# A fused two-block layer: the loads and first products of the ada prologue rearranged

## What is computed

```python
mod = (silu(c) @ w_ada + b_ada)                     # c: 1024, w_ada: 1024 x 6144
shift1, scale1, gate1, shift2, scale2, gate2 = split(mod, 6)
h = rms_norm(x, norm1_w) * (1.0 + scale1) + shift1  # x: 512 x 1024
proj = h @ w_in                                     # first product on h
```

## Time and profile before

| | us |
|---|---|
| median of three runs | 1274.04 |
| lowest and highest | 1273.92, 1275.78 |
| the profiled execution, device time | 1273.12 |
| its span | 1271.2 |
| PE busy | 1221.3 |
| DVE busy | 701.7 |
| ACT busy | 492.0 |

### The profile page before, as it was taken

The page is one execution under the profiler, slowest core; times in us unless marked ns, Lnnn a source line. Parts: engine busy times, 40 slices in busy tenths (PEclk is TensorE's granted clock), DMA queues, the critical chain, the costliest instruction groups (busy, mean ns, idle before and its releaser), DMA issues.

```text
span 1271.2 us, 20461 instructions
## 1 busy us (share of the span) xinstructions
PE 1221.3 (96%) x8672; PEld 994.5 (78%) x8672; DVE 701.7 (55%) x1018; ACT 492.0 (39%) x774; POOL 107.0 (8%) x151
## 2 busy tenths in 40 slices
PE   2899999997999999999999999999999999999998
PEld 2577788787878888888888889798767678888886
DVE  4699878654468544323333457758456546334344
ACT  4543543665246323112222344223446663232232
POOL 4000004621011000000000110000012320000000
PEclk9899999999999999999999999999999999999999
DMA  9666621000222535233322343333231115433311
GB/s 311 219 209 184 219 66 36 3 3 31 74 67 71 163 105 160 81 111 104 100 87 63 86 146 94 100 92 76 41 79 46 34 47 134 115 87 87 114 40 67
DMA packets 150955, 125.62 MB, mean 99 GB/s; under 512 B 16985, under 2 KB 134514, under 8 KB 150737
## 3 DMA queue, kind: packets, MB, share of 16 engines
q1 hardware_dynamic: 147888, 119.88, 31.3%
q0 software_dynamic: 1232, 2.07, 0.5%
q10 hardware_dynamic: 1744, 2.36, 0.5%
HBM read 122.20 MB, written 2.10 MB: 98 GB/s over the span
## 4 chain that ended last, share of the span: by engine, by line
PE 91%; DVE 3%; DMA 2%; ACT 2%; issue 1%; POOL 0%; ACTq 0%; DVEq 0%; POOLq 0%
PE bank L583 56%; PE bank L676 5%; PE bank L825 5%; PE bank L1255 4%; PE bank L1226 4%; PE bank L1289 3%; PE bank L1143 2%; DMA arena<-in_meta_tokens_dram 1%; PE bank L988 1%; PE bank L1117 1%; PE bank L834 1%; PE bank L1176 1%; PE bank L1198 1%; PE bank L1156 1%; PE bank L797 1%
## 5 line engine op out<-in xcount | busy, mean ns | idle before, releaser
L583 PE MATMUL bank<-hsplit,whi 128*128 128x512 f32 (+1 forms) x1872 | 551.9, 379 | 0.7 <-DVE wlo L2005 0.7
L583 PEld LDWEIGHTS bank<-hsplit,whi 128*128 128x128 f32 x1872 | 341.2, 188 | 73.0 <-issue 8.0
L583 PE MATMUL bank<-hsplit,wlo 128*128 128x512 f32 (+1 forms) x936 | 352.3, 376 | 0.0
L2005 DVE TENSOR_TENSOR wlo<-ring,whi 128x2048 fp32r<-128x2048 f32 (+4 forms) x97 | 196.9, 2029 | 178.1 <-ACT whi L1485 177.8
L1485 ACT ACTIVATE whi<-ring 128x2048 fp32r<-128x2048 f32 (+4 forms) x97 | 165.4, 1705 | 129.3 <-DVE xT L2355 53.3
L583 PEld LDWEIGHTS bank<-hsplit,wlo 128*128 128x128 f32 x936 | 175.9, 188 | 33.1
L583 PE MATMUL bank<-a_split,whi 128*128 128x512 f32 x340 | 104.6, 389 | 0.0
L583 PEld LDWEIGHTS bank<-a_split,whi 128*128 128x128 f32 x340 | 63.8, 188 | 13.2
L583 PE MATMUL bank<-a_split,wlo 128*128 128x512 f32 x170 | 66.1, 389 | 0.0
L2034 DVE SCALAR_TENSOR_TENSOR post<-ring,small,post 128x512 f32<-128x512 f32 x77 | 57.9, 752 | 3.1 <-DMA ring<-in_w_ada_dram 0.4
L1426 POOL TENSOR_TENSOR acc<-acc,tb 128x512 f32<-128x512 f32 x12 | 17.7, 1478 | 426.2 <-ACT tb L1723 426.2
(11 more groups left out here) (443 smaller groups left out, 1726.2 us busy)
## 6 DMA issues: line engine op xcount, KB each, us to landing
ring<-in_w_ada_dram SPq DMA_DIRECT2D x24, 1024.0 KB, 5.2
ring<-in_w_in_dram SPq DMA_DIRECT2D x22, 1024.0 KB, 5.3
ring<-in_w_in_dram SPq DMA_DIRECT2D x34, 512.0 KB, 5.1
ring<-in_w_gate_dram SPq DMA_DIRECT2D x11, 1024.0 KB, 5.4
ring<-in_w_up_dram SPq DMA_DIRECT2D x11, 1024.0 KB, 5.2
ring<-in_w_down_dram SPq DMA_DIRECT2D x8, 768.0 KB, 4.9
ring<-in_w_down_dram SPq DMA_DIRECT2D x8, 640.0 KB, 4.5
ring<-in_w_out_dram SPq DMA_DIRECT2D x4, 1024.0 KB, 5.3
```

The costliest lines, as they stand in the source:

```text
L583: last = mm(o[0:m, 0:n], w[:, k, c0:c0 + m], rhs(s, k), start=k + i == 0, stop=k == kn - 1 and i == 2)
L2005: split_lo = splitter(dve, None, lambda lo, src, hi: tt(lo, src, hi, ALU.subtract))
```

## The change

It touches the prologue only.

1. SP starts the load of `x` first, before all panels (ACT started it before). The eight half panels of ada blocks 2, 0, 3 and 1 get buffers of their own (`early_ada`, in memory that is used later) and semaphores of their own, and no longer pass through the ring. The order of SP is `x`, ada 2, ada 0, `qkv0`, ada 3, ada 1, `qkv1`, `qkv2`. `ld_const_rest` comes after `qkv2`.
2. Each of the four sums is shared: DVE takes the first half panel (four steps instead of eight), PE the second. PE takes each 128x128 piece of that half panel as stationary operand, with one column of silu(c) moving, 16 matmuls (`L630` in the changed kernel), and adds DVE's sum with the four matmuls that were there before. `ada_rows` and `ada_turn` are gone.
3. `scale1`, `shift1` and the modulation go by halves of the channels: blocks 2 and 0 for chunks 0 to 3, then blocks 3 and 1 for chunks 4 to 7. PE does ada 3 after chunk 1 of `first_tiles` and ada 1 after chunk 3.
4. `c` is loaded as eight rows of 128, turned by PE, and silu is applied from PSUM.
5. DVE copies chunks 0 to 3 of the transposed `x`, ACT chunks 4 to 7. The work on the meta tokens goes behind the first tiles, the memset of `gates` goes from DVE to POOL.

```diff
+        early_ada = {(i, h): hscratch[:, (2 * n + h) * PANEL:(2 * n + h + 1) * PANEL] for n, i in enumerate((2, 0)) for h in range(2)}
+        early_ada |= {half: C1.take(PANEL) for half in ((3, 0), (3, 1), (1, 0))}
...
+        early_ada[1, 1] = C1b.take(PANEL)
...
-        for i in range(4):
-            ada_panel(i)
...
             def ada(i):
 
                 o = open_tile(pe, "ada", i)
+                if i < 4:
+                    pe.wait_ge(*ada_loaded(i, 1))
+                    for k in range(4):
+                        for c in range(4):
+                            mm(o[:, c:c + 1], ada_half(i, 1)[:, k, c * P:(c + 1) * P], cs[:, 4 + k:5 + k],
+                               start=c + k == 0, stop=False)
                 pe.wait_ge(*done("adaacc", i))
                 for c in range(4):
-                    last = mm(o[:, c:c + 1], adaacc[i % 2][:, c * P:(c + 1) * P], ones[:, 0:1], start=True, stop=True)
+                    last = mm(o[:, c:c + 1], acc_of(i)[:, c * P:(c + 1) * P], ones[:, 0:1], start=i >= 4, stop=i >= 4 or c == 3)
                 last.then_inc(*fill("ada", i))
...
             pe.wait_ge(*arrived("const"))
-            pe.wait_ge(*arrived("x", 2))
+            pe.wait_ge(*arrived("c"))
+            tr(open_tile(pe, "c")[:, 0:KD], c_rows, ident[0:KD, 0:KD]).then_inc(*fill("c"))
+            pe.wait_ge(*arrived("x"))
...
+            ada(2)
+            norm_spread("1", diag)
             pe.wait_ge(*arrived("rows", 20))
...
-            ada(1)
-            norm_spread("1", diag)
...
-            ada_rows(3)
-            ada(2)
-            ada_turn(3)
+            ada(0)
...
-                    first_tiles("qkv0", h_ready("1"), [(("pj", c), P * c, T, hx) for c in range(2)])
+                    first_tiles("qkv0", h_ready("1"), [(("pj", c), P * c, T, hx) for c in range(2)],
+                                between={1: [(ada, 3)], 3: [(ada, 1)]})
+                    meta_columns()
...
+            sp.dma_start(x_in, a["x"][0].rearrange("(b p) f -> p b f", p=P)).then_inc(sem("ld_x"), 16)
+            load_ada(2)
+            load_ada(0)
             for i, (name, kn, width, parts) in enumerate(panels):
+                if name == "qkv1":
+                    load_ada(3)
+                    load_ada(1)
...
-            for k in range(KD):
+            for k in range(KD // 2, KD):
                 act.wait_ge(*filled("x", k))
                 A(xT[:, k, :], bank("x", k)[:, :], ACT.Copy).then_inc(*read("x", k))
...
-            modulate("1", modA1, 0)
+            modulate_half(0)
+            modulate_half(1)
...
+            ada_sum(2)
+            spread("1", diag)
             ada_sum(0)
...
+            normed("1", "xn1")
+            dve.wait_ge(*done("act_vectors", "v1"))
+            scale_half(0)
+            ada_mod(0)
+            split_lo()
+            h_rest("1", range(2))
+            ada_sum(3)
+            h_rest("1", range(2, 4))
             ada_sum(1)
+            scale_half(1)
+            ada_mod(1)
+            h_rest("1", range(4, 8))
```

More of the change, by code:

```diff
@@ L653, in _, with meta_columns @@
             tr(o[:, P:P + V2_N], rows2[0:V2_N, :], ident[0:V2_N, 0:V2_N]).then_inc(*fill("vec"))
[L654 to L661 removed]
+            ada(0)
+            def meta_columns():
+                pe.wait_ge(*arrived("meta"))
+                o = open_tile(pe, "meta")
+                for k in range(KD):
+                    last = tr(o[:, k * META:(k + 1) * META], meta_in[0:META, k * P:(k + 1) * P], ident[0:META, 0:META])
+                last.then_inc(*fill("meta"))
+                o = open_tile(pe, "spreadmeta")
+                pe.wait_ge(*done("dve_vectors", "diagmeta"))
+                mm(o[:, 0:META], ones[0:META, :], rbc[0:META, 0:META], start=True, stop=True).then_inc(*fill("spreadmeta"))
             hx = lambda s, k: h_even[:, s, k, :]
@@ L1500, in modulate, with modulate_half @@
                         hi_part("h" + tag, (k - 1,), h_of(tag, 0, k - 1), hpre[:, k - 1, :])
+            def modulate_half(half):
+                act.wait_ge(*done("modA1", half))
+                act.wait_ge(*copied("ada", half))
+                first = 4 * half
+                for k in range(first, first + 5):
+                    if k < first + 4:
+                        act.wait_ge(*done("xn1", k))
+                        A(hpre[:, k, :], hpre[:, k, :], ACT.Identity, scale=modA1[:, k:k + 1],
+                          bias=modT[:, k:k + 1]).then_inc(*signal("mod1", k))
+                    if k > first:
+                        act.wait_ge(*done("mod1", k - 1))
+                        hi_part("h1", (k - 1,), h_of("1", 0, k - 1), hpre[:, k - 1, :])
             def factor_out(tag):
@@ L1535, in _ @@
                     conv_in(m)
+                    if m == 1:
+                        act.wait_ge(*filled("meta"))
+                        A(hmeta, bank("meta")[:, 0:8 * META], ACT.Copy).then_inc(*read("meta"))
                     if m % 2:
@@ L2020, in ada_sum @@
             def ada_sum(i):
-                if i >= 2:
-                    dve.wait_ge(*filled("ada", i - 2 if i != 5 else 1))
-                acc = adaacc[i % 2]
-                for h in range(2):
-                    dve.wait_ge(*loaded(f"ada{i}{h}"))
-                    w = W(f"ada{i}{h}")
+                if i in (3, 1):
+                    dve.wait_ge(*filled("ada", 2 if i == 3 else 0))
+                elif i >= 4:
+                    dve.wait_ge(*filled("ada", {4: 3, 5: 1}.get(i, i - 2)))
+                acc = acc_of(i)
+                halves = 1 if i < 4 else 2
+                for h in range(halves):
+                    dve.wait_ge(*ada_loaded(i, h))
+                    w = ada_half(i, h)
                     for k in range(4):
@@ L2079, in raw_rest, with scale_half @@
                     .then_inc(*signal("raw" + tag, k))
-            dve.wait_ge(*done("act_vectors", "cs"))
-            ada_sum(0)
+            for k in range(KD // 2):
+                dve.wait_ge(*filled("x", k))
+                v.tensor_copy(xT[:, k, :], bank("x", k)[:, :]).then_inc(*read("x", k))
+            dve.wait_ge(*copied("c"))
+            ada_sum(2)
+            spread("1", diag)
+            ada_sum(0)
+            def scale_half(half):
+                ada_mod(2 + half)
+                dve.wait_ge(*copied("ada", 2 + half))
+                c = slice(4 * half, 4 * half + 4)
+                stt(out=modA1[:, c], in0=modT[:, 8 + 4 * half:12 + 4 * half], scalar=1.0, in1=col("norm1", 4 * half, 4),
+                    op0=ALU.add, op1=ALU.mult).then_inc(*signal("modA1", half))
+            for k in range(KD):
+                dve.wait_ge(*copied("x", k))
+            normed("1", "xn1")
[6 more added lines that the diff above has]
+            h_rest("1", range(2, 4))
             ada_sum(1)
-            dve.wait_ge(*arrived("const"))
-            spread("1", diag)
+            scale_half(1)
+            ada_mod(1)
+            h_rest("1", range(4, 8))
             dve.wait_ge(*done("act_vectors", "rootmeta"))
```

107 lines of the change are left out of this document (38 added, 69 removed).

## The result

| | before | changed |
|---|---|---|
| median, us (7 runs each) | 1274.01 | 1278.66 |
| lowest and highest | 1273.32, 1275.96 | 1275.71, 1279.51 |
| the profiled execution | 1273.12 | 1279.51 |
| its span | 1271.2 | 1277.3 |
| start of `qkv1` on PE (T) | 62.22 | 68.15 |

The medians differ by 4.65 us. The ratio, 1.003 with a 95% interval of 1.0018 to 1.0042, is 3.8 us, between 2.3 and 5.4: slower, clear of the noise. The forecast was 1279.8, slower by 5.8, with T at 68.6. The profiled execution of the changed kernel is the slowest of its seven.

The account below looks back on a forecast made before the run. PE, busy 96%, bounds; only T counts. The 13 us gained at the first product go to 13.5 of ada work, 2.9 of waiting and a clock lost twice more: T 62.3 to 68.6, 1279.8 us, range 1276 to 1284.

Parts of the forecast that it names:

- first product: Start of chunk 0 on PE: forecast at 35.9 us against 48.87 before, a gain of 13.
- gap ahead of chunk 4: PE idles 2.9 us for the second modulation after ada 1; this latency is now paid twice.
- own range: Time with ada groups and chunks between their two prices: 1276 to 1284 us, chance 0.58.
- the wide one: The range for 8 in 10, covering a faster outcome too: 1266 to 1284 us.
- rival 1: Narrow matmuls keep PE's granted clock: T 55.8, gain 6.5 us, time 1266.6; chance 0.22.
- The transposes: PE's transposes of x earn the clock; if the skill page were right, T would be 4.6 us later.
- ada 3 and ada 1: PE's ada groups after chunks 1 and 3, losing the clock within: 6.8 and 6.7 us.
- Chunks 0 to 3: First tiles on PE, between full and half clock: 4.0 us for chunks 0 and 1, 3.9 for 2 and 3.
- on the way: Chunks 0 and 1 start cold and the clock rises during them: 4.0 us, between 2.8 and 5.1.
- rival 2: ada 3 and ada 1 keep the clock: T 61.9, gain 0.4 us, time 1272.7; chance 0.16.
- 0.7 + 2.5 + 5.9: Landing of x from start, extra latency and transfer with constants: forecast at about 9.4 us.
- 3 us of cover, so nothing: Behind T, DVE's later meta scalings (1.2 us) cost nothing: qkv2's split was done at 70.2, used at 73.3.

Follow-up runs that it names:

- d_dve_whole: Changed kernel with DVE making the first four ada sums alone, PE only adding over partitions; 1272.15 us, 0.9989 against the kernel before.
- a_warm: Changed kernel plus two throwaway wide matmuls in each of PE's gaps, ahead of the first product and chunk 4; 1276.10 us, 1.0011 against before.
- g_both_early: Changed kernel with ada 1 moved from behind chunk 3 to directly behind ada 3; 1276.55 us, 1.0017 against the kernel before.
- e_loads_whole: Changed kernel's early loads, but qkv0 loaded after ada 1, computation undivided, DVE summing blocks 2, 0, 1; 1270.75 us, 0.9977 against before.
- b_warm: Kernel before the change plus five throwaway wide matmuls in PE's gap ahead of the first tiles; 1275.03 us, 1.0006 against before.
- h_two_rows_warm: e_loads_whole with ada 1 on PE with 512 columns and four throwaway wide matmuls ahead of the first tiles; 1269.84 us, 0.9970 against before.
- l_shared_row: h_two_rows_warm with ada 1 shared by DVE and PE, two fillers, and qkv3's split later on ACT; 1268.92 us, 0.9959 against before.
- c_wide: Changed kernel with PE's share of the ada sums done with 512 moving columns, the row copied by ACT; 1274.41 us, 1.0000 against before.

## Why the prediction was right, and where it was off

| step | forecast | measured |
|---|---|---|
| `x` landed | 9.4 | 10.1 |
| second half of ada 2 landed | 14.8 | 15.9 |
| ada 2 on PE | 5.9 | 5.2 |
| ada 0 on PE | 9.2 | 8.6 |
| ada 0 ends | 32.6 | 31.9 |
| first product | 35.9 | 35.1 |
| chunks 0 and 1 | 4.0 | 5.3 |
| ada 3 | 6.8 | 5.4 |
| chunks 2 and 3 | 3.9 | 5.1 |
| ada 1 | 6.7 | 5.6 |
| gap ahead of chunk 4 | 2.9 | 3.1 |
| chunks 4 to 7 | 7.5 | 8.0 |
| meta tokens | 0.9 | 0.8 |
| T | 68.6 | 68.15 |

**The mechanism held.** T decides: it moved by 5.9 us (forecast 6.3), the span by 6.1, the median by 4.65. The median of 1278.66 lies in the forecast's own range of 1276 to 1284, not only in the wide one that had to reach into rival 1. The first product came 13.8 us earlier, and ada work, a second gap and a lost clock spent it. The runs bear this out part by part. Without PE's share the change is 5 us faster (d_dve_whole), with the full clock in chunks 0 and 1 about 2.5 (a_warm), with the second gap closed about 2 (g_both_early, where part of the gap came back as half price); these last two are clear in T, not in the times. With neither share nor halves the new loads alone are worth 2.75 us (e_loads_whole, against its group's 1273.5).

**The clock.** The forecast took one-column matmuls for work that earns no clock and loses a granted one. Both are seen: PE was busy without a break from 20 to 31.9 at half clock (11.88 of 11.90 us), and each of the three groups that began at the full clock ended at half. Rival 1, the clock holds, is out. The Trainium skill, "TensorE: Matmul & The Clock Gate", under "Why this matters for your kernels", gives continuous work as the way to the full clock. This trace disagrees, with 100% busy and 0.50 from 28 to 30.

**The transposes** brought the clock again: ada 2, right behind them, ran at the full price (3.70 for its 16, where a group at half took 6.85). The Trainium skill, "TensorE: Matmul & The Clock Gate", Part 4, which the prediction weighed, says that the full clock doesn't engage for transposes. This trace disagrees.

**What was off** are the sizes of two terms, and they cancel: that T came out within 0.5 us is in part luck. ada 3 and ada 1 were put at 13.5 and took 11.0, since the fall comes late in the group: L630 still at 3.73 and 3.88, L634 at half. Chunks 0 to 3 were put at 7.9 and took 10.4. I let the clock rise "on the way" through two chunks. It rose when they were over, at about 40.3 and 50.5, so that each pair ran at half but for its last matmul, and the one-column matmuls behind it used what it had earned. For the same reason rival 2, with chunks 2 and 3 at 2.8, couldn't come: half of it (L630 at full price) was right.

**The loads** of `x` and ada 2 were 0.7 and 1.1 us late (the prediction's terms for `x`, 0.7 + 2.5 + 5.9, make 9.1 and not the 9.4 it went on with), and PE waited for the constants until 8.71 and for ada 2 0.8 us. The 0.7 us by which ada 2 was shorter made up for most of it.

**Behind T** the step "3 us of cover, so nothing" looked at the wrong queue. DVE's split was in time, but ACT's list has a split of a panel ahead of the square that PE needs; PE waited 0.2 us for it (L700). Here it is small because T was late. b_warm shows the full price, 2.9 us, when T comes early. A T of 55.8, as in rival 1, would likely have met the same queue and gained less than its 6.5 us; no run shows it.

## What to carry to other kernels

Share a sum with a matrix engine only where that engine would stand idle: here, inside its own bound stretch, even 5 us of narrow matmuls cost more than the vector engine's whole sum beside it. Where the bound engine's start is to be moved, count what lies between its first product and its steady stretch, and not when the first product comes. After a gain, look at the next queue that was just in time; an early start only pays once the loads and the order behind it allow it. A gap that can't be closed can be filled with wide matmuls whose result is thrown away, when the stretch behind it would begin at half clock. Begin it while the clock is still full: the fillers that did (b_warm, h_two_rows_warm) kept it, while of three that began at half (two in a_warm, one in l_shared_row) only one had the full clock by its end or soon after.

One profile is one execution. Before a time is read off a moment like T, compare what lies behind it as well: here it differed by 2 us and more between profiles, and once (d_dve_whole) the gain over the kernel before lay there.

## What the runs showed of the chip

- A granted clock didn't last through a group of 16 + 4 one-column matmuls in any of the changed kernel's three groups that began with it (L634 at their end at 1.64, 1.85 and 1.85 us, where 1.05 is the full price), though PE was never idle in them. The wide matmuls ahead of two of them (5.3 and 5.1 us at half) were over when the full clock came.
- In c_wide 2 us of small matmuls at the full price were followed by a chunk at half (1.11 for its first two matmuls, where the chunk before had 0.73).
- The code of the changed kernel up to the first product gave it at 35.07, 36.09 in g_both_early: the clock rose at another moment within the transposes of `x`, which took 5.08 and 6.04 us.
- With many 1 MB loads in the queue the issue itself takes time on SP: 0.5 to 5.9 us each in the changed kernel, against 0.37 for most of its later loads. Its rows of that line:

```profile
L1307 SPq DMA_DIRECT2D hscratch<-in_w_ada_dram x4: 492/1686/3711, 1.2 to 6.1; - x4
L1307 SPq DMA_DIRECT2D arena<-in_w_ada_dram x4: 1497/2376/5932, 11.9 to 21.6; - x4
```

  (ns: lowest, median, highest; then first and last start). SP had nothing else to do then, so it cost nothing here. A short load queued behind them on SP would have been issued later by as much.
